# Expert up weights issued by ScalarE on its own queue, gate and down weights by SyncE

## The reference

```python
def expert_choice_ffn(h, router_w, w_gate, w_up, w_down):
    B, n, D = h.shape
    cap = EC_CAPACITY * n // N_EXPERTS                      # 2 * 256 / 16 = 32
    aff = jax.nn.softmax((h @ router_w).astype(F32), axis=-1)
    gate, idx = lax.top_k(jnp.swapaxes(aff, 1, 2), cap)
    xe = jax.vmap(lambda hb, ib: hb[ib])(h, idx)
    a = jnp.einsum('becd,edf->becf', xe, w_gate)
    u = jnp.einsum('becd,edf->becf', xe, w_up)
    ye = jnp.einsum('becf,efd->becd', jax.nn.silu(a) * u, w_down) * gate[..., None].astype(h.dtype)
    return jax.vmap(lambda ib, yb: jnp.zeros((n, D), h.dtype).at[ib.reshape(-1)].add(yb.reshape(-1, D)))(idx, ye)
```

## Time and profile before

| what | before |
|---|---|
| median of 3 runs | 3221.33 us |
| the profiled execution | 3218.98 us |
| its span | 3217.2 us |
| granted TensorE clock, mean | 0.937 |
| TensorE matmul busy | 2834.0 us (88%) |
| VectorE busy | 1403.3 us (44%) |
| ScalarE busy | 472.7 us (15%) |
| bytes moved | 710.56 MB, 221 GB/s |
| issue to landing, median: in_moe_gate, in_moe_up, in_moe_down | 6.9, 10.6, 8.4 us |

### The profile page before, as it was taken

The page is one execution under the profiler, slowest core; times in us unless marked ns, Lnnn a source line. Parts: engine busy times, 40 slices in busy tenths (PEclk is TensorE's granted clock), DMA queues, the critical chain, the costliest instruction groups (busy, mean ns, idle before and its releaser), DMA issues.

```text
span 3217.2 us, 37133 instructions
## 1 busy us (share of the span) xinstructions
PE 2834.0 (88%) x14544; PEld 1854.5 (58%) x14544; DVE 1403.3 (44%) x2323; ACT 472.7 (15%) x958; POOL 39.4 (1%) x74
## 2 busy tenths in 40 slices
PE   6998998899999989979999959999998897877776
PEld 6685565676799668964545434555554384432332
DVE  6555341656577348764443442322223553211213
ACT  0001121100100121000000012121121061211211
POOL 1000000000000000000000000000000000000000
PEclk8998999999999999989999969999999898988988
DMA  6876322277655624561112135999998301899997
GB/s 212 296 267 245 118 79 92 69 275 275 209 184 186 232 76 154 196 212 43 59 63 74 53 105 246 380 382 387 373 389 347 118 14 66 370 422 422 422 422 303
DMA packets 249977, 710.56 MB, mean 221 GB/s; under 512 B 11789, under 2 KB 132637, under 8 KB 200088
## 3 DMA queue, kind: packets, MB, share of 16 engines
q1 hardware_dynamic: 240672, 677.42, 55.3%
q0 software_dynamic: 8384, 29.50, 2.8%
q10 hardware_dynamic: 832, 2.40, 0.2%
HBM read 708.13 MB, written 1.15 MB: 220 GB/s over the span
## 4 chain that ended last, share of the span: by engine, by line
PE 73%; DMA 14%; DVE 9%; issue 2%; ACT 1%; SPq 0%; ACTq 0%; DVEq 0%; POOL 0%
PE work L733 60%; DMA ring<-in_moe_up 11%; PE acc L733 11%; PE work L749 2%; DMA ring<-in_ffn_w_in 1%; DVE stats L1809 1%; DMA act_in<-in_cond_cols 1%; DMA prow<-mod_rows 1%; DVE rows_x L1788 0%; DVE rows_h L1826 0%; DVE rows_h L1820 0%; DVE stats L1775 0%; ACT cols_x L1363 0%; DVE scratch L2033 0%; DVE scratch L2028 0%
## 5 line engine op out<-in xcount | busy, mean ns | idle before, releaser
L733 PE MATMUL work<-ring,scratch 128*64 128x512 f32 (+2 forms) x3200 | 591.4, 628 | 120.1 <-DMA ring<-in_moe_up 60.3
L733 PE MATMUL work<-rows_h_parts,ring_parts 128*128 128x256 f32 x2816 | 522.9, 286 | 19.0 <-DVE cols_x_parts L1656 10.4
L733 PEld LDWEIGHTS work<-rows_h_parts,ring_parts 128*128 128x128 f32 x2816 | 448.8, 195 | 34.0 <-issue 33.1
L733 PEld LDWEIGHTS work<-ring,scratch 128*64 128x64 f32 (+2 forms) x3200 | 186.8, 130 | 480.4 <-issue 304.8
L733 PE MATMUL work<-cols_x_parts,ring_parts 128*128 128x256 f32 x1408 | 402.3, 286 | 0.0
L733 PE MATMUL work<-scratch 128*128 128x256 f32 (+3 forms) x1424 | 312.7, 369 | 21.6 <-ACT scratch L1478 11.1
L1667 DVE TENSOR_TENSOR ring_parts<-ring,ring_parts 128x2048 fp32r<-128x2048 f32 x132 | 302.6, 2292 | 4.5
L733 PEld LDWEIGHTS work<-scratch 128*128 128x128 f32 x1424 | 242.7, 193 | 84.1 <-ACT scratch L1478 38.6
L733 PE MATMUL work<-cols_x,ring 128*128 128x256 f32 (+1 forms) x896 | 283.0, 477 | 2.9 <-ACT cols_x L1363 2.0
L733 PEld LDWEIGHTS work<-cols_x_parts,ring_parts 128*128 128x128 f32 x1408 | 274.4, 195 | 0.9
L733 PEld LDWEIGHTS work<-cols_x,ring 128*128 128x128 f32 x896 | 172.6, 193 | 108.6 <-issue 94.3
(11 more groups left out here) (239 smaller groups left out, 2261.7 us busy)
## 6 DMA issues: line engine op xcount, KB each, us to landing
ring<-in_moe_gate SPq DMA_DIRECT2D x128, 1024.0 KB, 6.9
ring<-in_moe_up SPq DMA_DIRECT2D x128, 1024.0 KB, 10.6
ring<-in_moe_down SPq DMA_DIRECT2D x128, 1024.0 KB, 8.4
ring<-in_ffn_w_in SPq DMA_DIRECT2D x88, 1024.0 KB, 5.3
ring<-in_ada_w SPq DMA_DIRECT2D x48, 1024.0 KB, 7.4
ring<-in_ffn_w_out SPq DMA_DIRECT2D x44, 1024.0 KB, 6.6
ring<-in_xa_wkv SPq DMA_DIRECT2D x16, 1024.0 KB, 5.3
ring<-in_da_w_qkv SPq DMA_DIRECT2D x12, 1024.0 KB, 8.2
```

The lines of the kernel that those rows point to most:

```text
L733: ins = nc.tensor.matmul(o, lhsT, rhs, start=start, stop=stop, **kw)
```

## The change

The SyncE loop issues gate (loads base to base+3) and down (base+8 to base+11) alone. ScalarE's loop over the experts begins with the four DMAs of the up weights (base+4 to base+7), into the same slots, with the same wait on `loads_used` and the same landing semaphores, on ScalarE's queue. They stand ahead of the taken copy of the same expert. Slots, order of use and bytes are the same.

```diff
@@ SyncE, experts
-                    n = base
-                    for name in ("moe_gate", "moe_up", "moe_down"):
+                    for name, n in (("moe_gate", base), ("moe_down", base + 8)):
                         w = io[name][layer].rearrange("e k c -> (e k) c")
                         for quarter in range(4):
                             load(n, (2, D), w[bass.ds(e * D + quarter * 2 * P, 2 * P), :]
@@ ScalarE, experts, at the head of the loop's body
+                    up = io["moe_up"][layer].rearrange("e k c -> (e k) c")
+                    for quarter in range(4):
+                        n = base.loads + 4 + quarter
+                        act.wait_ge(loads_used, n + 1 + e * MOE_LOADS)
+                        act.dma_start(ring[:, n % RING, :].rearrange("p (a b) -> p a b", a=2),
+                                      up[bass.ds(e * D + quarter * 2 * P, 2 * P), :].rearrange("(p r) c -> p r c", r=2))\
+                            .then_inc(load_landed[n % RING], 16)
 
                     tk = taken[:, 0:KB * m].rearrange("p (k c) -> p k c", k=KB)
```

## The result

The changed kernel takes 3412.9 us (median of 4 runs, 3408.55 to 3416.41) against 3222.3 us before in the same runs: ratio 1.0591, 95% interval 1.0573 to 1.0610, slower by 190 us. The forecast was 3352 with a range of 3285 to 3395: the direction and the order of the loads are right, the size is 61 us short and outside the range.

What follows compares the result with a forecast made beforehand. Layer 0 was taken as bound by TensorE with the queues 90% full, layer 1 by the queues. Layer 0 +43, layer 1 +58 and clock +30 make +131 us on 3218.98: 3350, or 3352 on the median's scale; range 3285 to 3395.

Steps and rivals of the forecast that it cites:

- What bounds each stage, and the order of issues: Layer 0 bound by TensorE, layer 1 by queues; up issued at T0 (ScalarE's tile 10 copy ends), behind down.
- Half rate while both queues have work: Both layers: each queue gets half the bandwidth, so up's eight quarter times of 2.485 us take 19.9 us.
- rival B: Engines serve queues in order of arrival, up waits only for down: +2 layer 0, +13 layer 1; 3236 us; 10%.
- Moving from T0+1.5: Up's first bytes move 1.5 us after T0 (end of ScalarE's tile 10 copy), 1.4 us of it from the issue.
- In layer 0 ... no loss: Layer 0: TensorE stays busy 91% of a 35.7 us step, so the clock holds and costs nothing.
- The last expert counts as the others: Layer 0: SyncE's next-stage loads replace a seventeenth gate, so the last expert also loses 2.7 us.
- The clock in layer 1, 30 us: Layer 1: waits lower TensorE's clock, slowing the work behind them by 2.0 us a step, 15 times: 30 us.
- First experts: Four issues ahead of the copy TensorE awaits cost +1.9 us in layer 0; layer 1's first expert loses +6.
- A: Rival: the forecast mechanism in both layers without the clock loss, +101 us: 3322 us; chance 30%.
- C: Rival: two queues together move less than one, 380 GB/s, +2.2 us for 31 experts: 3420 us; chance 7%.
- D: Rival: two queues together move more than 422 GB/s; at 530 GB/s 3210 us, faster; chance 4%.
- E: Rival: up weights come no later in effect because ScalarE reaches the issues early: 3221 us; chance 4%.

Runs made afterwards that it cites:

- sp_up_last: Kernel before the change, with one queue, but SyncE issues gate, down, up, so up goes out after the last down: 3250.5 us (1.0095).
- gate_first: Changed kernel, but SyncE issues the next expert's gate ahead of this expert's down: 3345.0 us (1.0388).
- busy0_short: Changed kernel with two throwaway matmuls on TensorE ahead of the last up quarter in layer 0: 3401.3 us (1.0563).
- busy1_short: Changed kernel with three throwaway matmuls on TensorE ahead of each of up quarters 1 to 3 in layer 1: 3387.7 us (1.0516).
- act_mid: Changed kernel, but ScalarE issues the next expert's up behind its Silu, ahead of the copy of tile 10, and the first up ahead of the router: 3229.5 us (1.0028).
- sp_4kb: Changed kernel, but SyncE's gate and down loads come in runs of 4 KB instead of 8 KB (result differs, same bytes and work): 3287.5 us (1.0205).
- taken_first: Changed kernel with ScalarE's four up issues moved behind the taken copy: 3419.1 us (1.0612).

## Why the prediction was wrong in size

- **What bounds each stage, and the order of issues**: right. Up goes out at T0, behind down, and it is up that TensorE waits for in every step between the first and the last of a layer.
- **Half rate while both queues have work**: right, shown by 121 against 119 packets in 4 us and 576 against 604 from 3029.5 to 3049.5, and by moving the share with the packet size. This also decides between the forecast and rival B (order of arrival, 3236): sp_up_last has that order, in one queue, and took 3250, the changed kernel 3413.
- **"Moving from T0+1.5"**: the term that failed in layer 1. It put 1.4 us from the issue to the first bytes, wherever the other queue stood. On idle engines it is 1.0 (gate_first); with SyncE's packets ahead it is 3.5 (3025.98 to 3029.5), 3.4 to 3.7 in all later experts. So up lands at T0+24.2 and not T0+22.2, in 14 steps that were forecast at 34.8 us with the clock and took 36.85: 29 us. From T0 of the first expert to the end of the last one layer 1 lost 117.9 us where 52 + 6 + 30 = 88 were forecast, so this is nearly all of its error; the first expert is 2.3 us longer than forecast and the last 1.3 shorter.
- **"In layer 0 ... no loss" from the clock**: wrong, the second step that failed. The stretch at 85% busy and clock 1.00 said little about a step with its idle time in one or two waits, most of them 1.2 to 3.0 us long. The last quarter took up to 3.7 us where 1.94 is full speed. Layer 0 lost 71.1 us where 43 were forecast. Its 14 middle steps are 37.8 instead of 35.7; with a full clock (busy0_short) they are 36.3, so 1.5 of the 2.1 us are the clock. Of the last 0.6 some 0.4 are a later landing: the first bytes come late here too (T0+3.2 to T0+3.6), but down runs at full rate until then, and while up moves SyncE's queue sends only 365 to 506 packets beside its 512 (505 to 517 in layer 1). The other 0.2 are the last quarter, 1.94 standing alone where the sum had 1.74.
- **"The last expert counts as the others"** in layer 0: wrong, in the other direction. SyncE's next loads come in smaller packets and leave up(15) more than half of the bytes (from 2529 to 2535 us 0.37 MB in 186 packets beside 2.15 MB in 295): its last packet ends 18.8 us behind the issue, TensorE does not wait, and the step is 33.0 us (2518.29 to 2551.29), no loss where 2.7 were forecast.
- **The clock in layer 1, 30 us**: right; busy1_short gives 25 back, 1.8 us a step (36.85 to 35.03) against 2.0.
- **First experts**: +1.9 forecast for layer 0; the first taken copy came 2.4 us later behind its gather copy.
- **Rivals**: A (no clock loss) falls with busy1_short; C (two queues move less) with 426 GB/s while both run; D and E with the result. None had the late start, and none a clock loss in layer 0, which is why the range ended at 3395. (The 3320 to 3364 given for the two bounds of the clock are on the profiled execution's scale; on the median's they are 3322 to 3366, and nothing hangs on it.) A stall that repeats 31 times turns 1 us of doubt in a latency into 31 us; the range allowed for about that and no more.

The sum by its terms, then: 71 + 116 us in the steps from taken copy to taken copy, 5 us around them; of these 5, 2.7 had come before the first expert, for a reason that stays open. Of the steps' 187, some 37 go back with a full clock (25 + 12, by two runs; both at once was not run), and the rest is the wait for up at half rate, with its late start.

No version ran faster than the kernel before; act_mid, the best with two queues, is 8.7 us slower.

## To carry to other kernels

A load that moves to another engine's stream is issued when that engine gets there: look at what the engine waits for just ahead of that place, and whether loads with a later deadline now go out first. Two queues that share the DMA engines give up the order of one queue: the urgent load gets its share by packets, not by need, and starts later if the other queue already has loads in flight; issue it early enough (act_mid) or leave it in one queue. A stall of a few us in each pass of a loop costs more than itself, since the work behind it can run at half clock.

## What was not expected of the hardware

- The first bytes of a queue whose engines are busy with another queue came 3.4 to 3.7 us after the issue, against 1.0 on idle engines. With SyncE's packets at 4 KB instead of 8 KB it was 3.4 to 3.9 us, so it hardly goes with their size. Nor does it need SyncE to be issuing. In layer 1 of act_mid SyncE's last issue is 15 us old (rows below, then the queues from 2963 to 2964 us), and ScalarE's queue still starts 3.5 us late:

```profile
2942.25 3.67 SPq L626 DMA_DIRECT2D ring<-in_moe_gate  x4
2960.97 2.14 ACTq L1463 DMA_DIRECT2D ring<-in_moe_up  x4
2964.12 4.28 SPq L626 DMA_DIRECT2D ring<-in_moe_down  x4
...
q1 hardware_dynamic: 57, 0.40, 96.2%
```

  Counted from the packets, SyncE's queue moves 0.94 to 1.06 MiB between 1.0 us behind the issue and ScalarE's first packet in every later expert of the kernel after, in 120 to 136 packets of 8 KB, and about as much in sp_4kb (0.88 to 1.16 MiB), in 224 to 297 packets of 4 KB. That is one quarter's worth, and 2.5 us. Why that much goes first stays open.
- ScalarE's sequencer issues DMAs before activations that stand ahead of them in the program have begun (taken_first, where the table load held those up); in the changed kernel one issue took 0.34 us and four of them 2.1 us in all, with their waits and address arithmetic.
- One wait of 2.28 us in a step of 37 was enough for granted 0.58 in the 4 us from 2087 on, and yet four of the 14 middle steps kept the full clock, one of them behind 3.03 us. TensorE's window in the kernel after:

```profile
2087.00:2091.00 4.00, 3.75 (x10) 0.58 1.01 422
```
